# Even columns in one half, odd columns in the other: the layout of the rounded moving operands of a split-precision transformer kernel

## The chip, the cores and the metric

The kernel runs on one core of a Trainium2 chip. The metric is the device time of one execution in microseconds. The program computes three transformer blocks over 512 tokens and 1024 channels, in float32, in one launch.

## The reference

The reference is plain JAX. The first block has two layers, each a mixer and a squared-ReLU MLP; the second block has a SwiGLU, a mixer and a SwiGLU. Every one of them is a chain of matrix products, cut here to what matters:

```python
h = rms_norm(x, norm_mix[0])
qkv = h @ w_qkv                       # 1024 x 9216, then 3 groups of dilated attention, 8 heads
x = x + mixed.astype(h.dtype) @ w_o   # 1024 x 1024
h = rms_norm(x, norm_ffn[0])
a = jax.nn.relu(h @ w1)               # 1024 x 4096
x = x + (a * a) @ w2                  # 4096 x 1024
# layer 1: latent attention (w_in, w_qb, w_kvb, w_o), then the same MLP with other weights
# second block: (silu(g) * u) @ w_out, a mixer of differential attention and a gated recurrence,
# and (silu(g) * u) @ w_out again, each with an adaptive norm ahead and a norm behind
```

Float32 accuracy is wanted, and the weights are used once each: 385 units of 128x1024 numbers come from memory.

## The kernel before

**Tiles.** Activations lie with their channels on the 128 partitions and the 512 tokens along each partition, so a moving operand of TensorE is a row of 512 four-byte numbers in each partition. A weight unit (`raw`, 128x1024) holds eight 128x128 stationary tiles. A product of 1024 channels into one 128x512 PSUM bank takes eight such tiles.

**Split precision.** TensorE is fast on `float32r`, a rounded float32. So each number is used as a rounded high part plus a rounded rest. ScalarE writes the high part of the weights (`w_hi`, L1028), VectorE the rest (`w_lo`, L1685); activations are split the same way (`h_hi`/`h_lo`, `f_hi`/`f_lo`, `g_`, `s_`, `a_oh`/`a_ol`, `b_lh`/`b_ll`, `o_`, `r_`). `mm3` (L424) then issues three matmuls a tile: high by high (L426), high weight by low activation (L427), low weight by high activation (L428). All other products (attention scores, transposes, sums of squares by a matrix of ones) mostly use plain float32; the sums of squares in the first mixer (L507, L508) and the scores of the latent attention (L821 to L825) use the rounded form.

**Order.** Five programs are written out by hand, one for each engine, and meet at semaphores. SyncE loads units into four slots, each load released by the `lo` of three units before. ScalarE and VectorE split unit u+2 while TensorE multiplies unit u. `unit` (L430) waits once for its unit's `lo`; `unit_pair` (L439) works on two units at once, tile by tile, where the activations are just being made (behind a norm: VectorE `nrm` L1662, ScalarE `h_hi` L1071, VectorE `h_lo` L1655).

**What the change touches.** Reads: the moving operand of nearly every rounded matmul (`mm3`, L507, L508, L661, L662, L821 to L825). Writes: wherever a rounded activation, or the float32 tile it is split from, is made: `gained_high` L1075 and `gained_low` L1671, `norm` L1662, the squares of the first mixer L1102 and L1224, the attention outputs `a_oh`/`a_ol` (L1124, L1813) and `h_hi`/`h_lo` (L1427, L2066), the ReLU product `f_s` (L1872), the SwiGLU product `s_s` (L2174), the latents (L1943), keys (L1981, L1983), the recurrence's output (L1565, L2284), and the subln norm (L2310).

Of the kernel before, what the change touches and what calls it, by code (L numbers as in the profile page):

```python
# [19 lines left out]
ALU = mybir.AluOpType  # L20
# [93 lines left out]
def build(nc, stream, x_in, cols_in, crow_in, lam_in, pos_in, ada_in, gate_in, rope_in, consts_in, mask_in, out, stop="all"):  # L114
    with ExitStack() as ctx:
# [174 lines left out]

        class Halves:
# [129 lines left out]
        def _(pe):  # L421
            credits(pe, "mm", "A_T", "A_PV")

            def mm3(o, whi, wlo, xh, xl, start, stop):  # L424

                nc.tensor.matmul(o, whi, xh, start=start, stop=False)  # L426
                nc.tensor.matmul(o, whi, xl, start=False, stop=False)  # L427
                return nc.tensor.matmul(o, wlo, xh, start=False, stop=stop)  # L428
# [65 lines left out]
            def a_post(h, j, par):  # L494
# [8 lines left out]
                if j < 6:  # L503
# [3 lines left out]
                    nc.tensor.matmul(bank(7), ones_r[:], w_hi[:, 3, c], start=True, stop=False)  # L507
                    nc.tensor.matmul(bank(7), ones_r[:], w_lo[:, 3, c], start=False, stop=True).then_inc(S["A_ms"], 1)  # L508
# [147 lines left out]
            def first_sum(j, free):  # L656
# [4 lines left out]
                nc.tensor.matmul(bank(7), ones_r[:], w_hi[:, 3, c], start=True, stop=False)  # L661
                nc.tensor.matmul(bank(7), ones_r[:], w_lo[:, 3, c], start=False, stop=True).then_inc(S["A_ms"], 1)  # L662
# [56 lines left out]
            def b_key_tile(e):  # L719
                b_bank_free(e)  # L720
                sl = slot(U_BK)
                return mm3(bank(e % 4), tile_of(w_hi, sl, e), tile_of(w_lo, sl, e), b_lh[:, 0, :], b_ll[:, 0, :], True, True)
# [94 lines left out]
            def b_scores(h, r):  # L817
# [3 lines left out]
                nc.tensor.matmul(o, h_hi[:, h, c], b_kh[:, par, :], start=True, stop=False)  # L821
                nc.tensor.matmul(o, h_hi[:, h, c], b_kl[:, par, :], start=False, stop=False)
                nc.tensor.matmul(o, h_lo[:, h, c], b_kh[:, par, :], start=False, stop=False)
                nc.tensor.matmul(o, b_qs[:, par, c], b_krh[:, par, :], start=False, stop=False)
                nc.tensor.matmul(o, b_qs[:, par, c], b_krl[:, par, :], start=False, stop=True).then_inc(S["B_S"], 1)  # L825
# [192 lines left out]
        def _(act):  # L1018
# [54 lines left out]
            def gained_high(k, gain, to=h_hi):  # L1073

                A(to[:, k, :], x[:, k, :], ACT.Copy, scale=gain).then_inc(S["N_hi"], 1)  # L1075

            def a_head(h, par, project=True, attend=True, h0=0):

                more = (h - h0) * 3
                for j in range(9):  # L1080
                    n = 9 * h + j
                    if project:
# [15 lines left out]
                        if j < 6:  # L1098
# [3 lines left out]
                            A(sq[:, j % 2, :], a_raw[:, (par + j) % 2, :], ACT.Square).then_inc(S["A_sq"], 1)  # L1102
# [7 lines left out]
                    if attend:  # L1110
# [11 lines left out]
                        if j == 7:  # L1122
                            act.wait_ge(*after("A_PV", 4 * g + 3))
                            A(a_oh[:, bass.ds(g, 1), :].rearrange("p a n -> p (a n)"), bank(6), ACT.Copy).then_inc(S["A_oH"], 1)  # L1124
# [89 lines left out]
            def first_high(k):  # L1214
                act.wait_ge(S[f"x_in{k // 4}"], 16)
                A(a_oh[:, k, :], x[:, k, :], ACT.Copy, scale=col("norm_mix", k)).then_inc(S["E_hi"], 1)
# [1334 lines left out]
```

## Time and profile before

| | |
|---|---|
| median of 3 runs | 2503.85 us (2501.14 to 2504.0) |
| the profiled execution | 2502.02 us, span 2500.2 us |
| granted TensorE clock, mean | 0.997 |
| PE busy | 2446.2 us (98%), 11342 matmul records |
| PEld (weight load) busy | 1972.4 us (79%) |
| DVE busy | 1427.2 us (57%) |
| ACT busy | 1042.0 us (42%) |
| DMA | 249.57 MB, mean 100 GB/s |

The profiled execution is 1.8 us longer than its span, and 1.8 us under the median of the runs. PE is busy from end to end, but a record's own duration (389 ns for most) holds its way through the array, and the next one starts before it ends: what a matmul costs is the distance between two starts. A plain float32 matmul of 512 columns appears as two records.

### The profile page before, as it was taken

The numbers are of one execution on the slowest core, as the hardware profiler recorded it, in microseconds if no ns is written. First come the engines' busy times: TensorE is split into PE (matmuls) and PEld (weight loads), VectorE is DVE, ScalarE is ACT, GpSimd is POOL, SyncE is SP. The second block draws the span as 40 slices with busy tenths as digits, with TensorE's granted clock in tenths as the row PEclk, the third lists the DMA queues.
The fourth block names the chain that finished last, engine by engine and source line by source line (L and its number), as shares of the span: only waits on it lengthen the run. The fifth ranks groups of instructions, "written<-read, shape, count | busy, mean of one in ns | idle before, by whom it ended". The sixth has DMA issues, their size and how long they took to land.

```text
span 2500.2 us, 30958 instructions
## 1 busy us (share of the span) xinstructions
PE 2446.2 (98%) x11342; PEld 1972.4 (79%) x11342; DVE 1427.2 (57%) x2073; ACT 1042.0 (42%) x1562; POOL 0.2 (0%) x4
## 2 busy tenths in 40 slices
PE   7899999999999999999999999999999989999999
PEld 6788888878888886888888878888866666788886
DVE  6766666657565566857556564323356875432333
ACT  5555555543223246853223233222347554322233
POOL 0000000000000000000000000000000000000000
PEclk9999999999999999999999999999999999999999
DMA  4222222224344432024444423322322112223231
GB/s 156 68 76 76 75 75 75 76 87 167 128 152 158 160 112 73 1 77 151 160 143 143 169 80 108 98 98 87 108 68 72 55 43 68 90 89 108 86 108 68
DMA packets 71246, 249.57 MB, mean 100 GB/s; under 512 B 9824, under 2 KB 10336, under 8 KB 70752
## 3 DMA queue, kind: packets, MB, share of 16 engines
q1 hardware_dynamic: 68912, 247.28, 29.5%
q8 instruction: 74, 1.21, 0.2%
q10 hardware_dynamic: 2224, 0.79, 0.1%
q14 instruction: 36, 0.29, 0.0%
HBM read 245.94 MB, written 2.10 MB: 99 GB/s over the span
## 4 chain that ended last, share of the span: by engine, by line
PE 91%; DVE 5%; ACT 3%; issue 1%; DMA 0%; ACTq 0%; SPq 0%; DVEq 0%
PE psum L426 27%; PE psum L428 27%; PE psum L427 27%; PE psum L490 2%; PE psum L844 1%; PE psum L521 1%; PE psum L543 1%; PE psum L550 1%; DVE w_lo L1685 1%; PE psum L898 1%; PE psum L948 0%; DVE nrm L1662 0%; DVE x L2196 0%; PE psum L928 0%; DVE y L2194 0%
## 5 line engine op out<-in xcount | busy, mean ns | idle before, releaser
L426 PE MATMUL psum<-h_hi,w_hi 128*128 128x512 f32 x1768 | 701.7, 397 | 6.5 <-DVE w_lo L1685 3.8
L428 PE MATMUL psum<-h_hi,w_lo 128*128 128x512 f32 x1768 | 689.8, 390 | 0.0
L427 PE MATMUL psum<-h_lo,w_hi 128*128 128x512 f32 x1768 | 689.0, 390 | 0.0
L1028 ACT ACTIVATE w_hi<-raw 128x1024 fp32r<-128x1024 f32 x385 | 404.3, 1055 | 499.2 <-PE psum L428 489.1
L1685 DVE TENSOR_TENSOR w_lo<-raw,w_hi 128x1024 fp32r<-128x1024 f32 x385 | 465.8, 1219 | 149.0 <-ACT w_hi L1028 147.4
L426 PEld LDWEIGHTS psum<-h_hi,w_hi 128*128 128x128 f32 x1768 | 332.6, 188 | 83.3 <-issue 8.4
L428 PEld LDWEIGHTS psum<-h_hi,w_lo 128*128 128x128 f32 x1768 | 332.2, 188 | 70.9
L427 PEld LDWEIGHTS psum<-h_lo,w_hi 128*128 128x128 f32 x1768 | 332.6, 188 | 68.6 <-issue 2.6
L2174 DVE TENSOR_TENSOR s_s<-s_g,psum 128x512 f32<-128x512 f32 x44 | 30.2, 687 | 303.9 <-issue 241.1
L426 PE MATMUL psum<-f_hi,w_hi 128*128 128x512 f32 x512 | 199.2, 389 | 0.0
L427 PE MATMUL psum<-f_lo,w_hi 128*128 128x512 f32 x512 | 199.2, 389 | 0.0
L428 PE MATMUL psum<-f_hi,w_lo 128*128 128x512 f32 x512 | 199.2, 389 | 0.0
L426 PE MATMUL psum<-s_hi,w_hi 128*128 128x512 f32 x352 | 136.9, 389 | 0.0
L427 PE MATMUL psum<-s_lo,w_hi 128*128 128x512 f32 x352 | 136.9, 389 | 0.0
L428 PE MATMUL psum<-s_hi,w_lo 128*128 128x512 f32 x352 | 136.9, 389 | 0.0
L1157 ACT ACTIVATE f_r<-psum 128x512 f32<-128x512 f32 x64 | 38.2, 598 | 226.2 <-PE psum L428 226.1
L1899 DVE TENSOR_TENSOR nrm<-psum,rst 128x512 f32<-128x512 f32 x64 | 44.2, 690 | 146.1 <-PE psum L428 146.1
L426 PEld LDWEIGHTS psum<-f_hi,w_hi 128*128 128x128 f32 x512 | 96.1, 188 | 20.0
L428 PEld LDWEIGHTS psum<-f_hi,w_lo 128*128 128x128 f32 x512 | 96.1, 188 | 20.0
L427 PEld LDWEIGHTS psum<-f_lo,w_hi 128*128 128x128 f32 x512 | 96.1, 188 | 19.8
L1872 DVE TENSOR_TENSOR f_s<-f_r,psum 128x512 f32<-128x512 f32 x64 | 43.9, 685 | 118.8 <-ACT f_r L1157 118.8
L1182 ACT ACTIVATE s_g<-psum 128x512 f32<-128x512 f32 x44 | 26.3, 598 | 190.2 <-PE psum L428 190.2
(340 smaller groups left out, 3247.6 us busy)
## 6 DMA issues: line engine op xcount, KB each, us to landing
raw<-stream SPq DMA_DIRECT2D x385, 512.0 KB, 3.5
ada_raw<-ada_in SPq DMA_DIRECT2D x72, 512.0 KB, 4.1
x<-x_in SPq DMA_DIRECT2D x2, 1024.0 KB, 6.6
out<-x SPq DMA_DIRECT2D x8, 256.0 KB, 2.4
a_mask<-mask_in SPq DMA_DIRECT2D x1, 1024.0 KB, 9.4
crow<-crow_in SPq DMA_DIRECT2D x2, 512.0 KB, 4.5
gatew<-gate_in ACTq DMA_DIRECT2D x2, 256.0 KB, 3.9
a_cos<-rope_in SPq DMA_DIRECT2D x1, 256.0 KB, 7.7
```

Source lines behind the costliest of these rows:

```text
L426: nc.tensor.matmul(o, whi, xh, start=start, stop=False)
L427: nc.tensor.matmul(o, whi, xl, start=False, stop=False)
L428: return nc.tensor.matmul(o, wlo, xh, start=False, stop=stop)
L490: last = nc.tensor.transpose(o[:, b * P:(b + 1) * P], src[:, b * P:(b + 1) * P], ident[:])
L521: nc.tensor.matmul(psum[32 * t:32 * t + 32, 2 + r % 2, 0:256], q[:, 0, r * P + 32 * t:r * P + 32 * t + 32], a_k0[:, par, t * P:t * P + 256 ...
L1028: A(w_hi[:, slot(u0), :], raw[:, slot(u0), :], ACT.Copy).then_inc(S["hi"], 1)
L1157: A(f_r[:, j % 2, :], bank(j % 4), ACT.Relu).then_inc(S["F_r"], 1)
L1182: A(s_g[:, q % 2, :], bank(j % 6), ACT.Silu).then_inc(S["Sw_g"], 1)
L1685: V.tensor_tensor(w_lo[:, sl, :], raw[:, sl, :], f32(w_hi[:, sl, :]), ALU.subtract).then_inc(S["lo"], 1)
L1872: V.tensor_tensor(f_s[:, j % 2, :], f_r[:, j % 2, :], bank(j % 4), ALU.mult).then_inc(S["F_s"], 1)
L1899: V.tensor_tensor(nrm[:, 1, :], down, rst[:, 1, :], ALU.mult).then_inc(S["F_t"], 1)
L2174: V.tensor_tensor(s_s[:, q % 2, :], s_g[:, q % 2, :], bank((2 * jj + 1) % 6), ALU.mult).then_inc(S["Sw_s"], 1)
```

## The change

Three views are added. `stored(t)` names a row of 512 as two halves of 256; `by_parity(t)` names the same row's columns as the even ones, then the odd ones; `pairs(t)` reads a stored row as element 0 of the first half, element 0 of the second, element 1 of the first, and so on. A producer writes `stored(out)` from `by_parity(in)`: it reads at a step of two elements and writes two contiguous halves. TensorE reads `pairs(...)`, which gives it the columns in their old order, so PSUM and all behind it are as before. The rest `lo = value - hi` is taken between tiles that are both stored, or with one side read by parity. Only the first latent tile (`b_lh[:, 0]`), which is also a stationary operand, stays as it was; its matmuls (`b_key_tile`, `b_value_tile`) read plainly. No instruction is added, removed or moved on any engine; every instruction keeps its shape of 512 columns, its buffers and its waits.

```diff
+        def pairs(t):
+            return t.rearrange("p (a b) -> p b a", a=2)
+        def by_parity(t):
+            return t.rearrange("p (b a) -> p a b", a=2)
+        def stored(t):
+            return t.rearrange("p (a b) -> p a b", a=2)
...
-            def mm3(o, whi, wlo, xh, xl, start, stop):
+            def mm3(o, whi, wlo, xh, xl, start, stop, read=pairs):
+                xh, xl = read(xh), read(xl)
                 nc.tensor.matmul(o, whi, xh, start=start, stop=False)
                 nc.tensor.matmul(o, whi, xl, start=False, stop=False)
                 return nc.tensor.matmul(o, wlo, xh, start=False, stop=stop)
...
-                    nc.tensor.matmul(bank(7), ones_r[:], w_hi[:, 3, c], start=True, stop=False)
+                    nc.tensor.matmul(bank(7), ones_r[:], pairs(w_hi[:, 3, c]), start=True, stop=False)
...
-                return mm3(bank(e % 4), tile_of(w_hi, sl, e), tile_of(w_lo, sl, e), b_lh[:, 0, :], b_ll[:, 0, :], True, True)
+                return mm3(bank(e % 4), tile_of(w_hi, sl, e), tile_of(w_lo, sl, e), b_lh[:, 0, :], b_ll[:, 0, :], True, True, read=lambda t: t)
...
-                nc.tensor.matmul(o, h_hi[:, h, c], b_kh[:, par, :], start=True, stop=False)
+                nc.tensor.matmul(o, h_hi[:, h, c], pairs(b_kh[:, par, :]), start=True, stop=False)
...
-                A(to[:, k, :], x[:, k, :], ACT.Copy, scale=gain).then_inc(S["N_hi"], 1)
+                A(stored(to[:, k, :]), by_parity(x[:, k, :]), ACT.Copy, scale=gain).then_inc(S["N_hi"], 1)
...
-                            A(sq[:, j % 2, :], a_raw[:, (par + j) % 2, :], ACT.Square).then_inc(S["A_sq"], 1)
+                            A(stored(sq[:, j % 2, :]), by_parity(a_raw[:, (par + j) % 2, :]), ACT.Square).then_inc(S["A_sq"], 1)
...
-                A(h_hi[:, h, :], bank(4 + h % 2), ACT.Copy).then_inc(S["B_oH"], 1)
+                A(stored(h_hi[:, h, :]), by_parity(bank(4 + h % 2)), ACT.Copy).then_inc(S["B_oH"], 1)
...
-                    V.scalar_tensor_tensor(out=nrm[:, k % 2, :], in0=x[:, k, :], scalar=gain(k), in1=rst[:, 0, :],
+                    V.scalar_tensor_tensor(out=stored(nrm[:, k % 2, :]), in0=by_parity(x[:, k, :]), scalar=gain(k), in1=by_parity(rst[:, 0, :]),
                                            op0=ALU.mult, op1=ALU.mult).then_inc(S["N_s"], 1)
...
-                V.scalar_tensor_tensor(out=to[1][:, k, :], in0=x[:, k, :], scalar=gain, in1=f32(to[0][:, k, :]),
+                V.scalar_tensor_tensor(out=stored(to[1][:, k, :]), in0=by_parity(x[:, k, :]), scalar=gain, in1=stored(f32(to[0][:, k, :])),
                                        op0=ALU.mult, op1=ALU.subtract).then_inc(S["N_lo"], 1)
...
-                        V.tensor_tensor(f_s[:, j % 2, :], f_r[:, j % 2, :], bank(j % 4), ALU.mult).then_inc(S["F_s"], 1)
+                        V.tensor_tensor(stored(f_s[:, j % 2, :]), by_parity(f_r[:, j % 2, :]), by_parity(bank(j % 4)), ALU.mult).then_inc(S["F_s"], 1)
...
-                    V.tensor_tensor(s_s[:, q % 2, :], s_g[:, q % 2, :], bank((2 * jj + 1) % 6), ALU.mult).then_inc(S["Sw_s"], 1)
+                    V.tensor_tensor(stored(s_s[:, q % 2, :]), by_parity(s_g[:, q % 2, :]), by_parity(bank((2 * jj + 1) % 6)), ALU.mult).then_inc(S["Sw_s"], 1)
```

The other places (L661, L662, L822 to L825, L1124, L1216, L1224, L1565, L1697, L1709, L1813, L1943, L1981, L1983, L2066, L2284, L2310) are changed in the same two ways.

## Rows read from the trace of the kernel before

**Rows 1.** The page: span, busy time of each engine, and its chain by engine.
```profile
span 2500.2 us, 30958 instructions
PE 2446.2 (98%) x11342; PEld 1972.4 (79%) x11342; DVE 1427.2 (57%) x2073; ACT 1042.0 (42%) x1562; POOL 0.2 (0%) x4
PE 91%; DVE 5%; ACT 3%; issue 1%; DMA 0%; ACTq 0%; SPq 0%; DVEq 0%
```

**Rows 2.** Timeline of PE, two starts in the first MLP: start us, duration us.
```profile
700.01 0.39 PE L426 MATMUL psum<-h_hi,w_hi 128*128 128x512 f32 x1
...
705.45 0.39 PE L426 MATMUL psum<-h_hi,w_hi 128*128 128x512 f32 x1
```

**Rows 3.** Busy time by stretch, in the first MLP and in the first SwiGLU.
```profile
core 0: us, PE busy (x) PEld busy (x) DVE busy (x) ACT busy (x) POOL busy (x), PEclk, DMA share, GB/s
700.00:800.00 100.00, 100.00 (x443) 82.80 (x442) 57.81 (x78) 28.96 (x38) 0.00 (x0) 1.00 0.46 152
1600.00:1700.00 100.00, 100.00 (x443) 82.81 (x442) 32.20 (x34) 24.47 (x28) 0.00 (x0) 1.00 0.30 100
```

**Rows 4.** Chain in order of time, plain float32 matmuls: start us, us, records.
```profile
130.88 1.79 PE psum L550 x16
...
1887.56 3.43 PE psum L898 x8
```

**Rows 5.** One line's instructions, L426: duration min/median/max, first and last start.
```profile
L426 PE MATMUL psum<-h_hi,w_hi x1768: 387/389/799, 32.5 to 2424.6; 128*128 128x512 f32 x197
L426 PE MATMUL psum<-f_hi,w_hi x512: 389/389/389, 625.9 to 1480.3; 128*128 128x512 f32 x171
L426 PE MATMUL psum<-s_hi,w_hi x352: 389/389/389, 1609.7 to 2484.5; 128*128 128x512 f32 x176
L426 PE MATMUL psum<-g_hi,w_hi x256: 389/389/793, 1131.0 to 1436.8; 128*128 128x512 f32 x128
L426 PE MATMUL psum<-a_oh,w_hi x88: 389/389/796, 11.1 to 579.9; 128*128 128x512 f32 x88
L426 PE MATMUL psum<-b_lh,w_hi x32: 387/395/799, 955.0 to 994.2; 128*128 128x512 f32 x32
L426 PE MATMUL psum<-o_hi,w_hi x32: 389/389/628, 2054.9 to 2100.4; 128*128 128x512 f32 x32
L426 PE MATMUL psum<-r_hi,w_hi x32: 389/389/628, 2064.8 to 2103.1; 128*128 128x512 f32 x32
```

**Rows 6.** Groups by form: the other rounded matmuls (L508 as L507, L822-825 as L821).
```profile
L507 PE MATMUL psum<-w_hi,ones_r 128*128 128x512 f32 x42 | 16.3, 389 | 0.0
L821 PE MATMUL psum<-b_kh,h_hi 128*128 128x512 f32 x32 | 14.7, 460 | 0.0
L661 PE MATMUL psum<-w_hi,ones_r 128*128 128x512 f32 x6 | 2.5, 423 | 0.8 <-ACT rst L1056 0.8
```

**Rows 7.** Timeline of DVE at the first SwiGLU's norm: two tiles' first operation.
```profile
1489.81 0.75 DVE L1662 SCALAR_TENSOR_TENSOR nrm<-x,ada,rst 128x512 f32<-128x512 f32 x1
...
1491.26 0.75 DVE L1662 SCALAR_TENSOR_TENSOR nrm<-x,ada,rst 128x512 f32<-128x512 f32 x1
```

**Rows 8.** Groups by form on DVE and ACT: contiguous, and written at steps of four.
```profile
L1769 DVE TENSOR_TENSOR a_qk<-nrm,a_t 128x512 f32<-128x512 f32 x40 | 27.7, 692 | 1.4
L1766 DVE TENSOR_TENSOR a_k<-nrm,a_t 128x512 f32<-128x512 f32 x8 | 8.6, 1075 | 0.3
L1486 ACT ACTIVATE m_tmp<-psum 128x512 f32<-128x512 f32 x12 | 7.2, 599 | 12.3 <-PE psum L428 12.3
L1477 ACT ACTIVATE m_xr<-psum 128x512 f32<-128x512 f32 x4 | 4.4, 1093 | 3.3 <-PE psum L428 3.2
```

**Rows 9.** The page's groups: weight split, and the ReLU product.
```profile
L1028 ACT ACTIVATE w_hi<-raw 128x1024 fp32r<-128x1024 f32 x385 | 404.3, 1055 | 499.2 <-PE psum L428 489.1
L1685 DVE TENSOR_TENSOR w_lo<-raw,w_hi 128x1024 fp32r<-128x1024 f32 x385 | 465.8, 1219 | 149.0 <-ACT w_hi L1028 147.4
L1872 DVE TENSOR_TENSOR f_s<-f_r,psum 128x512 f32<-128x512 f32 x64 | 43.9, 685 | 118.8 <-ACT f_r L1157 118.8
```

More of the change, by code:

```diff
@@ L506, in a_post @@
                     c = slice((j % 2) * T, (j % 2 + 1) * T)
-                    nc.tensor.matmul(bank(7), ones_r[:], w_hi[:, 3, c], start=True, stop=False)
-                    nc.tensor.matmul(bank(7), ones_r[:], w_lo[:, 3, c], start=False, stop=True).then_inc(S["A_ms"], 1)
+                    nc.tensor.matmul(bank(7), ones_r[:], pairs(w_hi[:, 3, c]), start=True, stop=False)
+                    nc.tensor.matmul(bank(7), ones_r[:], pairs(w_lo[:, 3, c]), start=False, stop=True).then_inc(S["A_ms"], 1)
                 else:
@@ L660, in first_sum @@
                 c = slice((j % 2) * T, (j % 2 + 1) * T)
-                nc.tensor.matmul(bank(7), ones_r[:], w_hi[:, 3, c], start=True, stop=False)
-                nc.tensor.matmul(bank(7), ones_r[:], w_lo[:, 3, c], start=False, stop=True).then_inc(S["A_ms"], 1)
+                nc.tensor.matmul(bank(7), ones_r[:], pairs(w_hi[:, 3, c]), start=True, stop=False)
+                nc.tensor.matmul(bank(7), ones_r[:], pairs(w_lo[:, 3, c]), start=False, stop=True).then_inc(S["A_ms"], 1)
             def first_value(p, src, free=None):
@@ L820, in b_scores @@
                 o = bank(r % 2)
-                nc.tensor.matmul(o, h_hi[:, h, c], b_kh[:, par, :], start=True, stop=False)
[L822 to L825, printed above, removed]
+                nc.tensor.matmul(o, h_hi[:, h, c], pairs(b_kh[:, par, :]), start=True, stop=False)
+                nc.tensor.matmul(o, h_hi[:, h, c], pairs(b_kl[:, par, :]), start=False, stop=False)
+                nc.tensor.matmul(o, h_lo[:, h, c], pairs(b_kh[:, par, :]), start=False, stop=False)
+                nc.tensor.matmul(o, b_qs[:, par, c], pairs(b_krh[:, par, :]), start=False, stop=False)
+                nc.tensor.matmul(o, b_qs[:, par, c], pairs(b_krl[:, par, :]), start=False, stop=True).then_inc(S["B_S"], 1)
             def b_turn(m):
@@ L1123, in a_head @@
                             act.wait_ge(*after("A_PV", 4 * g + 3))
-                            A(a_oh[:, bass.ds(g, 1), :].rearrange("p a n -> p (a n)"), bank(6), ACT.Copy).then_inc(S["A_oH"], 1)
+                            A(a_oh[:, bass.ds(g, 1), :].rearrange("p a (c n) -> p (a c) n", c=2), by_parity(bank(6)), ACT.Copy).then_inc(S["A_oH"], 1)
             def outward(u0, rx, nn):
@@ L1215, in first_high @@
                 act.wait_ge(S[f"x_in{k // 4}"], 16)
-                A(a_oh[:, k, :], x[:, k, :], ACT.Copy, scale=col("norm_mix", k)).then_inc(S["E_hi"], 1)
+                A(stored(a_oh[:, k, :]), by_parity(x[:, k, :]), ACT.Copy, scale=col("norm_mix", k)).then_inc(S["E_hi"], 1)
             def first_square(k):
@@ L1223, in first_split @@
                 act.wait_ge(*after("A_ms", j - 2))
-                A(sq[:, j % 2, :], a_raw[:, j % 2, :], ACT.Square).then_inc(S["A_sq"], 1)
+                A(stored(sq[:, j % 2, :]), by_parity(a_raw[:, j % 2, :]), ACT.Square).then_inc(S["A_sq"], 1)
                 act.wait_ge(*after("A_sq", j))
@@ L1564, in m_rec_high @@
                 act.wait_ge(*after("M_ge", 2 * t + 1))
-                A(r_hi[:, t, :], m_gl[:, t, :], ACT.Copy, scale=0.5).then_inc(S["M_rh"], 1)
+                A(stored(r_hi[:, t, :]), by_parity(m_gl[:, t, :]), ACT.Copy, scale=0.5).then_inc(S["M_rh"], 1)
             for n in range(20):
@@ L1708, in first_norm @@
                     dve.wait_ge(*after("N_lo", k - 2))
[L1709 removed]
+                V.scalar_tensor_tensor(out=stored(nrm[:, k % 2, :]), in0=by_parity(x[:, k, :]), scalar=col("norm_mix", k), in1=by_parity(r0),
                                        op0=ALU.mult, op1=ALU.mult).then_inc(S["N_s"], 1)
@@ L1942, in b_latent_scaled @@
                 gain, src = (col("b_kv_a_gain"), 0) if t == 0 else (col("b_q_a_gain", t - 1), t + 1)
-                V.scalar_tensor_tensor(out=nrm[:, t % 2, :], in0=b_lat[:, src, :], scalar=gain, in1=rst[:, min(t, 1), :],
+                order = by_parity if t else stored
+                V.scalar_tensor_tensor(out=stored(nrm[:, t % 2, :]), in0=order(b_lat[:, src, :]), scalar=gain, in1=order(rst[:, min(t, 1), :]),
                                        op0=ALU.mult, op1=ALU.mult).then_inc(S["BI_s"], 1)
@@ L2283, in m_rec_low @@
                 dve.wait_ge(*after("M_rh", t))
-                V.scalar_tensor_tensor(out=r_lo[:, t, :], in0=m_gl[:, t, :], scalar=0.5, in1=f32(r_hi[:, t, :]),
+                V.scalar_tensor_tensor(out=stored(r_lo[:, t, :]), in0=by_parity(m_gl[:, t, :]), scalar=0.5, in1=stored(f32(r_hi[:, t, :])),
                                        op0=ALU.mult, op1=ALU.subtract).then_inc(S["M_rl"], 1)
```

19 lines of the change are left out of this document (10 added, 9 removed).

## The prediction

> **What bounds the kernel now.** I start at the page's chain by engine: PE holds 91% of the span, DVE 5%, ACT 3%, and PE is busy 98% of it [rows 1]. So only what TensorE does for each matmul can move this kernel far. Then the timeline of PE in a calm stretch, reading starts and not durations (389 ns is a matmul's way through the array, and each overlaps the next): from the start at 700.01 us to that at 705.45 us there are 24 matmuls [rows 2], so one costs 5.44 / 24 = 226.7 ns. Then the table by stretch, to see whether anything beside PE sets that pace: in the MLP VectorE is busy 57.8 of 100 us and DMA has a share of 0.46, in the SwiGLU 32.2 us and 0.30, and both stretches hold the same 443 matmul records at a granted clock of 1.00, which is the 2.4 GHz level [rows 3]. The pace is TensorE's own; it depends neither on the other engines nor on what comes from memory.
>
> The number itself is odd, and that is the heart of the case. 512 columns at 2.4 GHz are 213.3 ns. The plain float32 matmuls show what a matmul costs on top of its columns: eight records of L898 take 3.43 us on the chain [rows 4], 428.8 ns each, for 512 columns that are passed at half the rate (426.7 ns), so 2.1 ns on top. Records of 128 columns, L550, take 1.79 / 16 = 111.9 ns [rows 4] against 106.7 ns, so 5.2 ns on top. A rounded matmul pays 13.4 ns on top. Plain float32 takes one number of four bytes every 0.83 ns, the rounded form two. The 8 to 11 ns more appear only where the moving operand is read at the full rate, and loads of weights (128 columns, the same in both forms) stand beside both. I read this as a read of the moving operand that can't quite keep up, about one beat in 17 lost. The change alters exactly this read and nothing else on TensorE.
>
> **What the change costs and brings, part by part.**
>
> *Number of matmuls.* L426 has 1768 + 512 + 352 + 256 + 88 + 32 + 32 + 32 = 3072 [rows 5]. L427 and L428 have as many, and 8 of each line are the key tiles that keep the plain read: 3 x 3064 = 9192. L507 and L508 add 84, L661 and L662 12, and the scores of the latent attention 5 x 32 = 160 [rows 6]. Sum 9448.
>
> *The read in pairs.* The trace of before has no rounded matmul with another pattern than a contiguous row, so the effect must be bounded. Best end: the loss is gone and the on-top cost is that of L898, 2.1 ns: 215.4 ns, 11.3 ns less than now, 9448 x 11.3 ns = 107 us. With the 5.2 ns of L550 it is 218.5 ns, 8.2 ns less, 77 us. Worst end: two numbers that lie 1024 bytes apart can't be had in one beat, and the read falls to the pace of plain float32, 428.8 ns: 202.1 ns more, 1909 us. Middle: the loss is a cost per rounded matmul, whatever the pattern, and nothing changes. I take the best end with 2.1 ns, since L898 has the same 512 columns. The reason I lean to this side: in the contiguous row both numbers of one beat come from neighbouring addresses, in the new one each comes from its own contiguous half; a loss as regular as this one (the same in stages with wholly different load) looks like two reads at neighbouring addresses that get in each other's way, and that is what halves kept apart would end. That is an inference from one pace, and no row proves it.
>
> *Where TensorE's saving is not kept.* Behind the norms TensorE works at VectorE's pace: one tile takes VectorE 1491.26 - 1489.81 = 1.45 us [rows 7], and the six matmuls on it 6 x 226.7 ns = 1.36 us. In the four norms that lie open like this (the first one and the three of the second block, 8 tiles each) 4 x 48 = 192 matmuls save nothing: 2 us. The mixer of the second block has some waits of TensorE for softmax and recurrence; I take 2 us for it and the start. What is kept is 107 - 4 = 103 us.
>
> *The producers.* About 215 operations of VectorE and 100 of ScalarE now read at a step of two elements. In the trace of before such a step doesn't occur; a step of one costs VectorE 692 ns and a step of four 1075 ns, ScalarE 599 and 1093 ns [rows 8]. So an operation costs between nothing and 0.38 us (0.49 us) more. Where these lie beside TensorE's work they cost nothing even at the high end. The 64 ReLU products take 685 ns each and wait 118.8 us in all before them [rows 9]; in a unit of 24 x 215.4 ns = 5.17 us VectorE has 1.22 + 0.69 + 0.68 us of this and at most 1.22 us of the conditioning, 3.8 us, and with 0.38 us more 4.2 us. The splits of the weights wait for TensorE (489.1 us of ScalarE's idle time) and don't become late when a unit lasts 5.17 us instead of 5.44 [rows 9]. Open to the end lie the first operation of each tile in the four norms, 32 x 0.38 = 12 us at the high end, the eight first rests at the start, 3 us, and the last attention outputs and latents, 2 us: 0 to 17 us. Below nothing this can't be, since the step only takes reads apart. Of a step of two the row of one is the nearer to me, because two numbers are still within a distance that the row of four exceeds; I take 1 us.
>
> On that step this case has a rule to weigh. The row shows that at a step of 16 bytes VectorE takes 1.55 times as long [rows 8]. The Trainium skill, "Advanced Engine Details and Errata", Memory Cachelines, says that SBUF has lines of 16 bytes and wants at least two accesses on a line for full speed; at 8 bytes there are two, so by it the SBUF reads stay free. It says 8 bytes for PSUM, so that by it the reads of PSUM by parity (128 of VectorE, 16 of ScalarE) are slowed; nearly all of those lie under TensorE's work, and the sum would rise by under 2 us. No row of before shows a step of two.
>
> *Sum.* 2502.0 (the profiled execution) - 103 + 1 = 2400 us. The median of the runs is 1.8 us above that execution, so 2402 us.
>
> **The rivals.**
>
> 1. *Each number from another line: slower.* Place: the moving read of all 9448 matmuls. The pairs jump 1024 bytes forth and back at every number. For it: VectorE and ScalarE do pay for distant steps [rows 8], and TensorE has half the time per number that plain float32 has. Against it: the two places advance each in order, which a step of four does not. Price at the full end: 2502 + 1909 = 4411 us; it decides as soon as a pair costs more than the loss of now, that is at any pace over 226.7 ns, and each ns over it is 9.4 us.
> The cacheline rule of the Trainium skill (same page and section), taken for TensorE, speaks for this rival: the pairs never hit one line twice in a row. By it the pace would be the 428.8 ns of L898 and the time 4411 us. No row of before shows TensorE reading such a pattern.
>
> 2. *No change.* The 13.4 ns are a cost of each rounded matmul (switching weights, for instance), not of the read. For it: they are the same in every stage [rows 3]. Against it: the same weight loads stand beside L898, which pays 2.1 ns. Time: 2502 to 2507 us.
>
> 3. *No gain, and the producers' steps lie open.* Rival 2 with the high end of the producers: 2504 + 17 = 2521 us.
>
> 4. *Part of the gain.* The pace falls to 218 to 224 ns. With the 5.2 ns of L550 the sum is 2502 - 77 + 3 + 1 + 2 = 2431 us.
>
> **How the numbers follow.** Forecast with its own range, 2390 to 2435 us (which takes in the 2431 of rival 4): 0.64. A smaller gain, 2435 to 2498: 0.03. No change: 0.11. Rival 3: 0.04. Rival 1: 0.18. A measurement of this kernel tells about 0.2% (5 us) from no change. So faster 0.67, same 0.11, slower 0.22. The range goes from 2388 to 2522 us: it holds the forecast, the smaller gain, no change and rival 3, some 0.8, and leaves out rival 1, which lies far off.
>
> **What would show it.** In the changed kernel's timeline of PE the 24 starts of a unit should lie 5.17 us apart (215.4 ns each) instead of 5.44 us, in the MLP and in the SwiGLU alike, and about 464 records should stand in 100 us instead of 443. The durations should fall by the same 11 ns, from 389 to about 378. L898 and L550 should be as before. The key tiles' lines (b_lh) still read plainly and should keep 226.7 ns. The operations by parity should stay at 690 to 750 ns; if the ReLU product rises to 1000 ns, PSUM's step is dear and hidden. If starts are 429 ns apart, rival 1 holds. If they are 226.7 ns apart and the time is as before, the loss is not in the read, and my step on the best end is wrong.

## The result, and the profile after

| | before | after |
|---|---|---|
| median (lowest to highest), 4 runs each | 2503.07 us (2501.14 to 2504.0) | 2413.11 us (2411.46 to 2413.91) |
| the profiled execution, its span | 2502.02 us, 2500.2 us | 2412.52 us, 2410.7 us |
| granted TensorE clock, mean | 0.997 | 0.995 |

The ratio is 0.9641, with a 95% interval of 0.9624 to 0.9657: the changed kernel is 3.6% faster, 90 us. One of six later executions of after took 3524.54 us at a mean granted clock of 0.654 and is left out below. The forecast was 2402 us, and the time lies in the range of the likeliest case, 2390 to 2435 us. The name of a line in after is that of before plus 12 (L426 is L438), from about L300 to L1830.

The page of after: span, busy time, its chain by engine, and the costliest group (the columns behind the bar: busy us, mean ns of one, idle time before them and what ended it).

```profile
span 2410.7 us, 30958 instructions
PE 2348.6 (97%) x11342; PEld 1987.2 (82%) x11342; DVE 1458.4 (60%) x2073; ACT 1055.3 (44%) x1562; POOL 0.2 (0%) x4
PE 88%; DVE 6%; ACT 3%; issue 2%; DMA 0%; ACTq 0%; SPq 0%; DVEq 0%
L438 PE MATMUL psum<-h_hi,w_hi 128*128 128x512 f32 x1768 | 684.4, 387 | 9.1 <-DVE w_lo L1697 4.5
```

Against [rows 1]: as many instructions, and PE still bounds. But its own part of the chain has fallen from 91% to 88%, and that of VectorE has risen from 5% to 6%; VectorE and ScalarE have 31 and 13 us more of busy time for the same operations.

The timeline of PE in after, two starts 24 matmuls apart in the first MLP (start us, duration us):

```profile
700.03 0.38 PE L439 MATMUL psum<-f_lo,w_hi 128*128 128x512 f32 x1
...
705.21 0.38 PE L439 MATMUL psum<-f_lo,w_hi 128*128 128x512 f32 x1
```

24 starts take 5.18 us, 215.8 ns each, where [rows 2] had 226.7 ns. The chain in order of time shows the plain float32 matmuls (start us, us, records) as they were in [rows 4], 1.79 and 3.43 us:

```profile
129.06 1.79 PE psum L562 x16
...
1814.59 3.43 PE psum L910 x8
```

The table by stretch of after, against [rows 3]: the first row lies in the first MLP, the second in the first SwiGLU.

```profile
core 0: us, PE busy (x) PEld busy (x) DVE busy (x) ACT busy (x) POOL busy (x), PEclk, DMA share, GB/s
700.00:800.00 100.00, 100.00 (x465) 87.55 (x465) 59.65 (x79) 27.91 (x35) 0.00 (x0) 1.00 0.45 155
1550.00:1650.00 100.00, 100.00 (x465) 87.58 (x464) 35.19 (x37) 24.75 (x27) 0.00 (x0) 1.00 0.29 100
```

465 records stand where 443 stood, in both stages. And the kernel holds its own control: the key tiles of the latent attention read as before, the query tiles after them in pairs, with the same buffers (timeline of PE, first and last matmul of 12 key tiles' matmuls, then of 12 of the query tiles'):

```profile
916.71 0.40 PE L438 MATMUL psum<-b_lh,w_hi 128*128 128x512 f32 x1
...
919.25 0.39 PE L440 MATMUL psum<-b_lh,w_lo 128*128 128x512 f32 x1
...
932.18 0.38 PE L438 MATMUL psum<-b_lh,w_hi 128*128 128x512 f32 x1
...
934.56 0.38 PE L440 MATMUL psum<-b_lh,w_lo 128*128 128x512 f32 x1
```

11 steps take 2.54 us (231 ns each) on the plain read and 2.38 us (216 ns) on the pairs. In before the same 11 steps of the key tiles take 2.49 us. The way of reading makes the difference between the two, with all else alike.

What is not as forecast are the producers. Groups by form in after (mean ns of one is the number behind the comma):

```profile
L1884 DVE TENSOR_TENSOR f_s<-f_r,psum 128x512 f32<-128x512 f32 x64 | 54.5, 852 | 93.0 <-ACT f_r L1169 92.9
L1674 DVE SCALAR_TENSOR_TENSOR nrm<-x,ada,rst 128x512 f32<-128x512 f32 x24 | 20.5, 864 | 9.8 <-ACT rst L1070 9.2
L1087 ACT ACTIVATE h_hi<-x,cols 128x512 fp32r<-128x512 f32 x16 | 15.4, 965 | 0.0
L1439 ACT ACTIVATE h_hi<-psum 128x512 fp32r<-128x512 f32 x8 | 4.7, 588 | 1.2 <-PE psum L856 1.2
L1825 DVE TENSOR_TENSOR a_ol<-psum,a_oh 128x512 f32 x6 | 4.2, 692 | 0.1
```

The first three read SBUF at a step of two and take 852 ns (685 in [rows 9]), 864 and 965 ns. The last two read only PSUM at that step and take 588 and 692 ns, what [rows 8] has for a step of one.

### The profile page after: what moved, and what is told of

Read it like the earlier page. It is cut to its first block, busy times and chain, and to the rows that moved or that the text cites. A ratio compares the mean times of both kernels' runs of the same rounds, so it can differ in the third digit from the quotient of the medians.

```text
span 2410.7 us, 30958 instructions
## 1 busy us (share of the span) xinstructions
PE 2348.6 (97%) x11342; PEld 1987.2 (82%) x11342; DVE 1458.4 (60%) x2073; ACT 1055.3 (44%) x1562; POOL 0.2 (0%) x4
## 4 chain that ended last, share of the span: by engine, by line
PE 88%; DVE 6%; ACT 3%; issue 2%; DMA 0%; ACTq 0%; SPq 0%; DVEq 0%
PE psum L438 26%; PE psum L439 26%; PE psum L440 26%; PE psum L502 2%; PE psum L856 1%; DVE w_lo L1697 1%; PE psum L555 1%; DVE nrm L1674 1%; PE psum L533 1%; PE psum L562 1%; PE psum L910 1%; PE psum L960 0%; DVE x L2211 0%; DVE h_lo L1667 0%; ACT w_hi L1040 0%
## 5 line engine op out<-in xcount | busy, mean ns | idle before, releaser
L438 PE MATMUL psum<-h_hi,w_hi 128*128 128x512 f32 x1768 | 684.4, 387 | 9.1 <-DVE w_lo L1697 4.5
L439 PE MATMUL psum<-h_lo,w_hi 128*128 128x512 f32 x1768 | 671.2, 380 | 0.0
L440 PE MATMUL psum<-h_hi,w_lo 128*128 128x512 f32 x1768 | 671.0, 380 | 0.0
L1697 DVE TENSOR_TENSOR w_lo<-raw,w_hi 128x1024 fp32r<-128x1024 f32 x385 | 466.5, 1221 | 139.6 <-ACT w_hi L1040 138.0
L438 PEld LDWEIGHTS psum<-h_hi,w_hi 128*128 128x128 f32 x1768 | 335.1, 190 | 69.3 <-issue 9.6
L440 PEld LDWEIGHTS psum<-h_hi,w_lo 128*128 128x128 f32 x1768 | 334.8, 189 | 47.8
L2189 DVE TENSOR_TENSOR s_s<-s_g,psum 128x512 f32<-128x512 f32 x44 | 37.1, 843 | 276.1 <-issue 218.7
L438 PE MATMUL psum<-f_hi,w_hi 128*128 128x512 f32 x512 | 194.0, 379 | 0.0
L439 PE MATMUL psum<-f_lo,w_hi 128*128 128x512 f32 x512 | 194.0, 379 | 0.0
L440 PE MATMUL psum<-f_hi,w_lo 128*128 128x512 f32 x512 | 194.0, 379 | 0.0
L438 PE MATMUL psum<-s_hi,w_hi 128*128 128x512 f32 x352 | 133.4, 379 | 0.0
L440 PE MATMUL psum<-s_hi,w_lo 128*128 128x512 f32 x352 | 133.4, 379 | 0.0
L1884 DVE TENSOR_TENSOR f_s<-f_r,psum 128x512 f32<-128x512 f32 x64 | 54.5, 852 | 93.0 <-ACT f_r L1169 92.9
L440 PEld LDWEIGHTS psum<-f_hi,w_lo 128*128 128x128 f32 x512 | 96.8, 189 | 13.7
L438 PEld LDWEIGHTS psum<-f_hi,w_hi 128*128 128x128 f32 x512 | 96.8, 189 | 13.7
```

The source lines that it names most:

```text
L1697: V.tensor_tensor(w_lo[:, sl, :], raw[:, sl, :], f32(w_hi[:, sl, :]), ALU.subtract).then_inc(S["lo"], 1)
L1884: V.tensor_tensor(stored(f_s[:, j % 2, :]), by_parity(f_r[:, j % 2, :]), by_parity(bank(j % 4)), ALU.mult).then_inc(S["F_s"], 1)
L2189: V.tensor_tensor(stored(s_s[:, q % 2, :]), by_parity(s_g[:, q % 2, :]), by_parity(bank((2 * jj + 1) % 6)), ALU.mult).then_inc(S["Sw_s"], 1)
```

## The experiments

Two theories stood at the start. A "beat" is here, as in the prediction, the 0.83 ns in which the rounded form passes two numbers; that the two are read together is the picture behind the theories, and no row shows it. A, the one on record: the 11 ns come from the moving read, whose two numbers of a beat got in each other's way at neighbouring addresses. B: the 13.4 ns on top belong to each rounded matmul or to its weight load. Beside these: what do the slower producers cost, and why are they slower? The median of before in the three groups of runs below was 2501.7, 2501.05 (a single run) and 2501.96 us. Kernels with a single time below were run once; what is read from them is the pace. A pace is always that of starts in a calm stretch, read as in [rows 2].

**Only the read in pairs.** The producers write as they did before; the columns come in another order, so the output is that of permuted tokens.

```diff
         def by_parity(t):
-            return t.rearrange("p (b a) -> p a b", a=2)
+            return stored(t)
```

> The changed kernel with the producers put back to contiguous reads and writes; only TensorE's moving reads stay in pairs. Its columns come out in another order than the reference's, so this run tells time alone. Theory (the whole gain is the pace of the moving read, and the producers' step of two takes a part of it back): the pace stays 215.8 ns and the time lies under the 2413 us of the changed kernel, at 2402 to 2407 us. Rival (the producers cost nothing, and the missing part of the forecast gain is waits that TensorE's faster pace exposes): the same 2413 us.

Measured: 2407.58 us (2404.27 to 2409.65, 4 runs), ratio 0.9623, interval 0.9607 to 0.9639; pace 215.8 ns. The median lies just above the 2402 to 2407 us of the theory, and clearly under the rival's 2413. The producers in this kernel, groups by form:

```profile
L1884 DVE TENSOR_TENSOR f_s<-f_r,psum 128x512 f32<-128x512 f32 x64 | 43.8, 685 | 102.1 <-ACT f_r L1169 102.0
L1674 DVE SCALAR_TENSOR_TENSOR nrm<-x,ada,rst 128x512 f32<-128x512 f32 x24 | 17.8, 750 | 9.8 <-ACT rst L1070 9.2
L1087 ACT ACTIVATE h_hi<-x,cols 128x512 fp32r<-128x512 f32 x16 | 11.3, 707 | 0.0
```

They are back at 685, 750 and 707 ns. The step of two costs after 5.5 us by the medians (2413.1 - 2407.6), 8.2 us by the spans of the profiled executions (2410.7 - 2402.5). By stage, from the starts of the first matmuls: 2.6 us lie in the dilated attention, 1.0 in the latents and scores, 2.9 in the second block's mixer, 0.9 in each SwiGLU, and none in the MLPs. But this profiled execution is the fastest of its four, at a mean clock of 0.997; the other three took 2406.72 to 2409.65 us at 0.994 to 0.996, while after has 0.995 in all four. By these means after is at the 1.2 GHz level for some 24 us (2410.7 x 0.005 / 0.5) and this execution for 14 us (2402.5 x 0.003 / 0.5). At half the rate, 10 us more are worth about 5 us, an estimate. So most of the 8.2 us may be the clock, and the 5.5 us of the medians are the better figure for the producers.

**Only the producers' step of two.** TensorE reads plainly; the output is permuted again.

```diff
         def pairs(t):
-            return t.rearrange("p (a b) -> p b a", a=2)
+            return t
```

> The changed kernel with TensorE reading every moving operand contiguously; the producers still read by parity and write two halves. Columns come out in another order, so this run tells time alone. Theory: the pace of rounded matmuls goes back to 226.7 ns and the time to 2505 to 2512 us, a little above the kernel before. Rival (it is the place at which the columns are stored that helps, not the order of reading): the pace stays at 216 ns. On the producers: if they are slow because TensorE's paired reads get in their way, the ReLU product falls back to 685 ns and the scaling behind the norm to 751 ns; if the step of two alone does it, they stay at 850 to 900 ns.

Measured: 2502.14 us (2501.45 to 2504.78, 10 runs), ratio 1.0002, interval 0.9993 to 1.0012; pace 226.7 ns. The same groups, and one more of ScalarE:

```profile
L1884 DVE TENSOR_TENSOR f_s<-f_r,psum 128x512 f32<-128x512 f32 x64 | 43.8, 685 | 118.8 <-ACT f_r L1169 118.7
L1674 DVE SCALAR_TENSOR_TENSOR nrm<-x,ada,rst 128x512 f32<-128x512 f32 x24 | 17.8, 751 | 9.8 <-ACT rst L1070 9.2
L1087 ACT ACTIVATE h_hi<-x,cols 128x512 fp32r<-128x512 f32 x16 | 11.9, 747 | 0.0
L1114 ACT ACTIVATE sq<-a_raw 128x512 f32<-128x512 f32 x42 | 28.5, 679 | 1.9
```

The time is that of before, not the 2505 to 2512 us expected. This was the surprise. With a plain read beside it, VectorE's step of two costs nothing at all (685 and 751 ns), ScalarE's 40 ns (707 to 747). Neither half of the change slows VectorE alone; only both together do: 685 to 852 ns, 750 to 864 ns. In after itself the eight first rests (L1709) take 743 to 753 ns, as in before, and the same operation later (L1683), beside TensorE's pairs, 899 ns. Four of the eight run before TensorE's first matmul; the other four run beside pairs, but there the matmuls start 0.43 us apart, at half the calm pace. So pairs alone don't slow VectorE either. The slow operations lie beside pairs at full pace, and no run has that pace with another pattern: whether the pattern or the pace does it is open.

**Half the columns.** In before, the third matmul of `mm3` works on its first 256 columns only (its product is left incomplete). A cost per beat would fall by half in it, a cost per matmul would not.

```diff
-                return nc.tensor.matmul(o, wlo, xh, start=False, stop=stop)
+                return nc.tensor.matmul(o[:, 0:256], wlo, xh[:, 0:256], start=False, stop=stop)
```

> The kernel before, with the third matmul of each triple (low weight by high activation) on the first 256 columns only; the rest of that product is left out. It tells whether the 13.4 ns on top of 213.3 ns are paid per matmul or per column. Theory (a loss in the read, proportional to columns): the half matmuls follow each other at 106.7 + 6 to 8 = 113 to 115 ns. Rival (a fixed cost of each rounded matmul): 106.7 + 13.4 = 120 ns. The full ones keep 226.7 ns in both.

Measured: 2231.66 us. Timeline of PE (start us, duration us):

```profile
699.96 0.28 PE L428 MATMUL psum<-h_hi,w_lo 128*128 128x256 f32 x1
700.09 0.39 PE L426 MATMUL psum<-h_hi,w_hi 128*128 128x512 f32 x1
700.32 0.40 PE L427 MATMUL psum<-h_lo,w_hi 128*128 128x512 f32 x1
700.55 0.28 PE L428 MATMUL psum<-h_hi,w_lo 128*128 128x256 f32 x1
```

Averaged over a calm stretch, the three steps are 229.3, 233.3 and 124.1 ns. Their columns alone would take 213.3, 213.3 and 106.7 ns; on top lie 16, 20 and 17 ns, 53 in all where three whole ones have 40. Neither theory said that the two whole neighbours would get dearer. The run is inconclusive on A against B. It made me suspect the load of weights, about 188 ns long, which now lies over other columns than before; the two runs with the weights at a step of two test that.

**Step of two.** In before, the moving operand of `mm3` is read as even columns, then odd ones (permuted output): every number of a beat in another place, 8 bytes on.

```diff
+        def view(t):
+            return t.rearrange("p (b a) -> p a b", a=2)
...
             def mm3(o, whi, wlo, xh, xl, start, stop):
+                xh, xl = view(xh), view(xl)
```

> The kernel before, with the moving operands of each triple stored contiguously and read at a step of two columns: all even ones, then all odd ones. Columns come out in another order. Theory (two numbers at neighbouring addresses get in each other's way, and 1024 bytes apart they don't): at 8 bytes apart nothing is gained, the pace is 226.7 ns or more. Rival (any departure from the contiguous row ends the loss): 216 ns. Second rival (each beat needs its two numbers from one 8-byte word or from two fixed halves): a clearly slower pace, up to 429 ns.

Measured: 4551.23 us. Timeline of PE (start us, duration us):

```profile
999.85 0.63 PE L430 MATMUL psum<-a_oh,w_hi 128*128 128x512 f32 x1
1000.30 0.63 PE L431 MATMUL psum<-a_ol,w_hi 128*128 128x512 f32 x1
1000.75 0.63 PE L432 MATMUL psum<-a_oh,w_lo 128*128 128x512 f32 x1
1001.21 0.63 PE L430 MATMUL psum<-a_oh,w_hi 128*128 128x512 f32 x1
```

The starts are 0.45 us apart (451 ns in a calm stretch): twice the 226.7 ns of the plain row. The price of my rival 1 is real, but for a step of two, not for pairs from two halves.

**Pairs at other distances.** The same edit with `"p (g a b) -> p g b a"`, a=2, and b = 4 (numbers 16 bytes apart), b = 16 (64 bytes), and b = 2 (8 bytes: 0, 2, 1, 3 within one group of 16 bytes); and fours from four quarters, `"p (a b) -> p b a"` with a=4. All in before's `mm3`, with permuted output.

> The kernel before, with the moving operands of each triple stored contiguously and read in pairs 16 bytes apart: columns 0 and 4, 1 and 5, 2 and 6, 3 and 7, then the next eight. Columns come out in another order. Theory A (a beat's two numbers must either be neighbours or lie in different banks, and banks change every few bytes): full pace, 216 to 227 ns. Theory B (only far apart halves are read at full pace; near ones collide as the step of two did at 452 ns): about 430 to 452 ns.

> As the run with pairs 16 bytes apart, but 64 bytes apart (columns 0 and 16, 1 and 17, and so on, then the next 32). Theory A: 216 ns. Theory B: 430 to 452 ns unless 64 bytes already count as far; the pair of both runs shows from which distance the pace is full.

> As the run with pairs 16 bytes apart, but 8 bytes apart: columns 0 and 2, 1 and 3, then 4 and 6, 5 and 7. Columns come out in another order. Theory (both numbers of a beat must be neighbours in one 8-byte word, or lie 16 bytes or more apart): the pace falls to about 452 ns as with the step of two, which also takes numbers 8 bytes apart. Rival (it is the change from one pair to the next that counts, not the distance within a pair): 216 ns.

> The kernel before with moving operands read in fours, 512 bytes apart each: columns 0, 128, 256, 384, then 1, 129, and so on. Columns come out in another order. Theory A (a beat's two numbers must lie in different banks, however the pattern goes on): 216 ns as with pairs. Theory B (what counts is that each of two streams goes on contiguously from beat to beat, as with two halves; here each beat's pair changes place): slower than 216 ns, up to 430 to 452 ns.

Measured: 2408.35, 2408.55, 2501.71 and 2983.67 us, at 215.8, 215.8, 226.7 and 283 ns a matmul. The table by stretch of the four kernels (columns as above), 16 bytes first:

```profile
700.00:800.00 100.00, 100.00 (x465) 87.56 (x464) 59.31 (x80) 27.91 (x35) 0.00 (x0) 1.00 0.46 153
```

64 bytes:

```profile
700.00:800.00 100.00, 100.00 (x465) 87.55 (x464) 59.47 (x80) 27.91 (x35) 0.00 (x0) 1.00 0.46 152
```

8 bytes:

```profile
700.00:800.00 100.00, 100.00 (x443) 82.81 (x442) 57.66 (x79) 30.45 (x41) 0.00 (x0) 1.00 0.47 156
```

Fours:

```profile
700.00:800.00 100.00, 100.00 (x355) 67.41 (x354) 44.61 (x61) 21.25 (x28) 0.00 (x0) 1.00 0.37 129
```

Of the distances tried, 16 bytes are enough, and more brings nothing: halves 1024 bytes apart are no better. At 8 bytes the expectation was missed: the pace is exactly that of the contiguous row. So it is not only numbers side by side that cost. What all three full-pace patterns have, and the contiguous row and the 8-byte pairs lack, is that a beat's two numbers never lie in one group of 16 bytes. But that is not enough. The fours have it too, and theory A had them at 216 ns; they are slower than the contiguous row. And the step of two has the same pair as the 8-byte run, columns 0 and 2, but goes on to another group of 16 bytes at the next beat, where that run stays for 1 and 3: 451 against 226.7 ns. What follows from beat to beat counts as well.

**The weights at a step of two.** In before, the stationary tile takes every second of 256 columns (the product is another one); the moving read stays plain. If the load takes part in the loss, it moves the pace.

```diff
         def tile_of(t, sl, w):
-            return t[:, sl, w * P:(w + 1) * P]
+            return t[:, sl, w // 2 * 2 * P:(w // 2 + 1) * 2 * P].rearrange("p (m two) -> p two m", two=2)[:, w % 2, :]
```

> The kernel before with plain moving reads, but each 128x128 stationary tile is taken as every second column of 256, so that the weight load reads at a step of two. Output channels come out in another order. Theory (the 13.4 ns on top are a collision of the moving read with the load of the next weights, which the half columns made likelier): another pattern of the weight load moves the pace of the moving read off 226.7 ns, either way, and the load lasts longer than 188 ns. Rival (the loss lies within the moving read): the pace stays 226.7 ns.

Measured: 2560.02 us; pace 233.3 ns, 6.6 ns dearer, with the moving read untouched. The group of weight loads, and the stretch:

```profile
L426 PEld LDWEIGHTS psum<-h_hi,w_hi 128*128 128x128 f32 x1768 | 343.6, 194 | 83.6 <-issue 8.1 <-DVE h_lo L1655 3.1 <-ACT a_raw L1231 1.8
700.00:800.00 100.00, 100.00 (x431) 82.70 (x430) 58.19 (x81) 28.94 (x38) 0.00 (x0) 1.00 0.48 161
```

A load takes 194 ns (188 in before), still less than the step between two matmuls. It is not the load's length that sets the pace. How the weights lie moves the pace of a plain read.

**Both: weights at a step of two, moving read in pairs** (the first kernel of this section with the edit above; its product is another one too).

> The run with the read alone in pairs, and the stationary tiles taken at a step of two columns as in the run that moved the plain pace from 226.7 to 233.3 ns. Columns and channels come out in another order. Theory (the loss is a collision of the plain moving read with the load of the next weights, and a read in pairs doesn't meet it): the pace stays 215.8 ns in spite of the step of two in the weight load, time about 2405 us. Rival (pairs mend another loss, and the weights' pattern adds its own 6.7 ns): 222 ns and 2468 us.

Measured: 2407.97 us, pace 215.8 ns, as without the edit (2407.58). The stretch:

```profile
700.00:800.00 100.00, 100.00 (x465) 90.88 (x464) 58.20 (x78) 27.89 (x35) 0.00 (x0) 1.00 0.47 155
```

The loads have become longer here too (90.9 us of 100, against 87.6), and it costs nothing. The step of two in the weights is worth 6.6 ns beside a plain row and nothing beside pairs. It is tempting to read this as a collision of the contiguous moving read with the load of the next weights, which the pairs don't meet. The two runs show less: the weights' layout matters to one read and not to the other.

**Matmuls with no load beside them.** The traces also speak against the load as the cause of the 10.85 ns. Where TensorE stops behind a triple, its last matmul has no load beside it: its own was done before it began, and the next comes after its read. In after, one such matmul of L440 reads plainly (the key tile at 919.25 us) and one in pairs (a query tile, 936.71 us). The next load (timeline of PEld) and the duration of the matmul (group by form, mean ns of one), first for the plain one, then for the pairs:

```profile
920.17 0.19 PEld L438 LDWEIGHTS psum<-b_lh,w_hi 128*128 128x128 f32 x1 [0.96 <-ACT b_kn L1324]
L440 PE MATMUL psum<-b_lh,w_lo 128*128 128x512 f32 x1 | 0.4, 388 | 0.0
938.37 0.30 PEld L498 LDWEIGHTS psum<-b_qr,rotm 128*128 128x128 f32 x2 [1.68 <-ACT b_qr L1329]
L440 PE MATMUL psum<-b_lh,w_lo 128*128 128x512 f32 x1 | 0.4, 379 | 0.0
```

With loads beside them these durations are 389 and 379 ns. Before has 29 matmuls of this kind at the 2.4 GHz level, none under 388 ns and 26 of them at 388; after has 52 in pairs, all at 379. And where the next instruction starts right behind (L508 to L521 in before, L520 to L533 in after, seven places each), it starts 318 to 319 ns after the plain matmul and 309 to 310 ns after the one in pairs.

So some 9 of the 10.85 ns are there with no load beside the read: they belong to the read itself. The ends of matmuls in a trace are modelled, but these starts are not ends. The layout of the weights adds to a plain read, and not by the next load alone: in the kernel with weights at a step of two, all but one of the matmuls of L428 without a load beside them take 397 ns, and those of L508, whose own tile is contiguous, 388 ns. (Such a duration is not fixed by the two layouts alone: in the run with pairs 16 bytes apart, where L508's read is still plain, it is 397 ns.)

**The residual stored in halves.** The runs pointed to a better version: PSUM is read by parity for nothing, SBUF is not. So the residual streams themselves are kept as halves; each change of order is made where a value comes out of PSUM, and the norms, `h_hi`, `h_lo` and `f_s` read contiguous SBUF. The whole reference is computed. Three of its edits:

```diff
-                A(stored(to[:, k, :]), by_parity(x[:, k, :]), ACT.Copy, scale=gain).then_inc(S["N_hi"], 1)
+                A(to[:, k, :], x[:, k, :], ACT.Copy, scale=gain).then_inc(S["N_hi"], 1)
...
-                        A(f_r[:, j % 2, :], bank(j % 4), ACT.Relu).then_inc(S["F_r"], 1)
+                        A(stored(f_r[:, j % 2, :]), by_parity(bank(j % 4)), ACT.Relu).then_inc(S["F_r"], 1)
...
-                    V.tensor_tensor(x[:, o, :], x[:, o, :], bank(o % 4), ALU.add).then_inc(S["R_x"], 1)
+                    V.tensor_tensor(stored(x[:, o, :]), stored(x[:, o, :]), by_parity(bank(o % 4)), ALU.add).then_inc(S["R_x"], 1)
```

> A version that computes the whole reference: the changed kernel, with the residual x and the outputs y kept in the stored order (the input and the output are laid out so outside the chip), and with the change of order made where PSUM is read (ReLU, SiLU, residual sums, y). Norms, gained high and low parts read SBUF contiguously again. Theory (step-two reads of SBUF are slowed while TensorE reads in pairs, step-two reads of PSUM are not): the scaling behind the norm falls from 903 to 751 ns, the ReLU product from 849 to 687 ns, and the time from 2413 to 2405 to 2408 us, as with the read alone. Rival (PSUM reads by parity become dear when there are so many of them): 2413 us or more.

> The changed kernel itself once more, on the same chip as the version with the stored residual, to compare the two: 2411 to 2414 us.

Measured: 2409.61 us (2408.35 to 2410.12, 5 runs), ratio to before 0.9629, interval 0.9617 to 0.9641. After, again on the same chip: median 2412.03 us of five runs between 2411.72 and 2414.1 us, ratio 0.9642, interval 0.9629 to 0.9654. The two intervals overlap, the runs themselves don't: 2.4 us, 0.1%, for the new version. It is the fastest full kernel here, but misses the 2405 to 2408 us expected. Its producers, groups by form:

```profile
L1887 DVE TENSOR_TENSOR f_s<-f_r,psum 128x512 f32<-128x512 f32 x64 | 43.8, 685 | 102.1 <-ACT f_r L1172 102.0
L1677 DVE SCALAR_TENSOR_TENSOR nrm<-x,ada,rst 128x512 f32<-128x512 f32 x24 | 17.8, 751 | 9.8 <-ACT rst L1073 9.2
L1117 ACT ACTIVATE sq<-a_raw 128x512 f32<-128x512 f32 x42 | 33.1, 788 | 1.8
```

`f_s` still reads its bank by parity beside TensorE's pairs and takes 685 ns: its read of PSUM doesn't take part in this. The squares of the first mixer (788 ns) still read SBUF at a step of two. By stage, the second block's mixer (2.0 us less than after) and the two SwiGLUs (0.9 us each) gain, and the dilated attention has 0.6 us more than after (508.3 against 507.7). 5.3 us over the read alone are left in the span (2407.8 - 2402.5), 3.3 us of them in the dilated attention. The mean clock of this execution is 0.995 and that of the read alone 0.997, so here too most of the 5.3 us may be the clock.

## Why the prediction was right, and where it was not

**What bounds the kernel: right.** TensorE's own pace does. The MLPs keep all of it: 1536 matmuls at 10.85 ns are 16.7 us, and the two MLPs are 16.6 and 16.7 us shorter.

**The size of the pace: right, 0.4 ns off.** Forecast 215.4 ns, measured 215.8 ns. 9448 x 10.85 ns = 102.5 us instead of 107. That it came so close is in part luck: the 2.1 ns on top were borrowed from L898, which reads at half the rate, and nothing in before showed that pairs would reach them.

**Its cause: right in the place, unproven in the middle.** The place was the moving read, and there the loss is: the loads, buffers and waits are the same in both kernels, and 9 of the 10.85 ns are there without a load beside the read. The step behind it was: "a loss as regular as this one [...] looks like two reads at neighbouring addresses that get in each other's way". No run shows that. Pairs 8 bytes apart, no longer neighbours, gain nothing, so it could at best hold for numbers within 16 bytes; and the fours, 512 bytes apart, are slower than the contiguous row. Which accesses get in each other's way stays open.

**Rival 2: wrong, with one thing in it that I had at nothing.** It had the 13.4 ns as a cost of each rounded matmul whatever the read; with pairs 2.5 ns of them are left. It named "switching weights", and the weights do matter to a plain read (226.7 to 233.3 ns when they lie at a step of two) and not to pairs. I set the loads aside because the same ones stand beside L898, which pays 2.1 ns. But L898 takes its numbers at half the rate, so that row could exclude a cost of the load alone, not a disturbance of the read.

**Rival 1: right as a danger, wrong for this pattern.** A step of two is the half rate (451 ns), fours are 283 ns; pairs from two halves are the full rate. The cacheline rule of the Trainium skill ("Advanced Engine Details and Errata", Memory Cachelines), taken for TensorE, made the pairs the slow case. The traces disagree in both directions: a step of 8 bytes has two numbers on a line of 16 and costs 451 ns, and pairs that never hit one line twice in a row cost 215.8 ns.

**What is not kept of the saving: more than I took.** I took 4 us. With the producers as in before, the profiled execution is 97.7 us shorter than before (2502.0 - 2404.3), 4.8 us less than 102.5; the medians on that chip differ by 94.1 us (2501.7 - 2407.6), 8.4 us less. In after it comes to more, since the second block's mixer keeps nothing: 185.4 us for its input stage where before had 185.2, 69.3 us for its output stage where before had 69.5, where 672 matmuls would give 7 us. The table by stretch there, in before:

```profile
2006.00:2092.00 86.00, 78.59 (x368) 60.50 (x367) 58.21 (x83) 49.55 (x84) 0.00 (x0) 0.98 0.20 64
```

and in after:

```profile
1932.00:2020.00 88.00, 78.73 (x368) 63.36 (x367) 58.85 (x83) 49.29 (x82) 0.00 (x0) 0.92 0.19 66
```

The same number of records, 368, takes 88 us instead of 86. PE is busy for as long, though each matmul is shorter: the granted clock is 0.92 of the full 2.4 GHz on average instead of 0.98, that is some 14 us at 1.2 GHz (88 x 0.08 / 0.5) instead of 3 (86 x 0.02 / 0.5). At half the rate, these 11 us more would account for some 5.5 of the 7 us, an estimate from the two rows. With the read alone 3 of the 7 us are kept (183.4 and 68.3 us), and the clock there is 0.96:

```profile
1926.00:2012.00 86.00, 77.04 (x368) 62.12 (x367) 58.44 (x82) 48.91 (x83) 0.00 (x0) 0.96 0.21 64
```

No run separates TensorE's waits from its clock: whether the waits lower the clock here is open.

**The producers: the mis-sized term.** I took 1 us of 0 to 17, with each operation at its step-of-one duration. They are 5.5 us by the medians; the 8.2 us of the spans hold the clock too, as worked out above. One tile of a norm now takes VectorE 1.60 us, where [rows 7] has 1.45. Two starts of the timeline of DVE (start us, duration us):

```profile
1435.29 0.90 DVE L1674 SCALAR_TENSOR_TENSOR nrm<-x,ada,rst 128x512 f32<-128x512 f32 x1
...
1436.89 0.90 DVE L1674 SCALAR_TENSOR_TENSOR nrm<-x,ada,rst 128x512 f32<-128x512 f32 x1
```

32 open tiles at 0.15 us are 4.8 us, most of the 5.5. (The bounds of the range came from [rows 8], where the step of four is one of writing, and the change reads at a step; a read at a step of four in before, L2278, takes 1088 ns, much the same.) The guess at the step itself was right (685 and 751 ns with the producers' part alone); what I missed is that it does not stay so beside pairs at full pace. By the place in the Trainium skill named above, reads of SBUF at 8 bytes would be free and reads of PSUM dear. The traces agree for SBUF beside a plain read on VectorE (685 and 751 ns), and nowhere else: ScalarE pays 40 ns for it, beside pairs it is 852 to 965 ns, and PSUM at that step is free (692 and 588 ns). That the ReLU product would stay hidden was right: the MLPs lose nothing with 852 ns.

**The sum again, with measured terms:** 2502.0 - 102.5 + 4.8 + 8.2 = 2412.5 us, the profiled execution. It closes by construction, since 4.8 and 8.2 are differences of profiled executions. Of the 11 us between forecast and median, 4.5 are the pace and 8.0 the unkept part and the producers together (13.0 instead of 5), less 1.2 us: I added 1.8 us from the profiled execution to the median, and it was 0.6 us. How the 8.0 divide depends on what is compared: 0.8 and 7.2 by the profiled executions; by the medians, which come from different chips, 4.4 and 4.5. All these errors lie within the range of 2390 to 2435 us, which was wide enough for them.

## What to carry to other kernels

Where TensorE bounds a kernel of rounded float32 products with a weight load at each, read the step between starts, subtract columns divided by clock, and if much is left over, try another pattern of the moving read; here a view that takes the two numbers of each beat from places 16 bytes or more apart gave 10.85 of 13.4 ns back, with no added instruction. Don't let TensorE read a whole row at a step of two: that costs double (451 ns). Make any change of order where a value is read out of PSUM, since other engines' strided reads of SBUF became slower just beside the pairs; here that was worth 2.4 us more.

## What the runs showed of the hardware that I had not expected

- The pace of a rounded matmul of 512 columns depends on how both operands lie in SBUF: contiguous row 226.7 ns, the same with weights at a step of two 233.3 ns, pairs 16, 64 or 1024 bytes apart 215.8 ns (the last with either layout of the weights), pairs 8 bytes apart 226.7 ns, fours 283 ns, a step of two 451 ns.
- The loss of the plain row does not need a load of weights beside it: 388 ns against 379 ns for a matmul with none, 389 against 379 ns with one.
- Operations of VectorE and ScalarE that read SBUF at a step of two slow down beside pairs at full pace, and hardly beside a plain read: `f_s` 685 to 852 ns, `h_hi` 747 to 965 ns. Reading PSUM at that step costs nothing beside pairs (692 and 588 ns).
- Not settled: what in the plain row costs 10.85 ns, why the layout of the weights adds to it and not to pairs, and why the strided reads of the other engines slow down beside pairs. The runs show which patterns are slow together, not by what part of the chip.
